# Seven sub-products of a gated layer in another order, passes of 6, 8 and 8 tiles, and one subtraction moved from VectorE to GpSimd

## What is computed

```python
def trunk(x, ...):
    for l in range(DEPTH):                                  # DEPTH = 2
        x = x + 0.5 * swiglu(rmsnorm(x, norm_g[l, 0]), ffn_w_gu[l, 0], ffn_w_down[l, 0])
        xn = rmsnorm(x, norm_g[l, 1])
        y, ns = even_mixer(xn, ...) if l % 2 == 0 else odd_mixer(xn, ...)
        x = x + y
        x = x + 0.5 * swiglu(rmsnorm(x, norm_g[l, 2]), ffn_w_gu[l, 1], ffn_w_down[l, 1])
    return rmsnorm(x, final_norm_g), new_states

def swiglu(x, w_gu, w_down):                                # 1024 -> 2 x 2816 -> 1024
    g, u = jnp.split(x @ w_gu, 2, axis=-1)
    return (jax.nn.silu(g) * u) @ w_down
```

## Time and profile before

| | |
|---|---|
| median of 3 runs | 2731.59 us (2727.64 to 2732.09) |
| the profiled execution | 2732.55 us, span 2730.8 us |
| mean granted TensorE clock | 0.959 |
| PE / VectorE / ScalarE / GpSimd busy | 94% / 60% / 35% / 29% of the span |
| an undisturbed up-tile | 12.31 us |

### The profile page before, as it was taken

How to read it: one execution, slowest core, us unless ns; L and a number is a source line. 1 busy time by engine, 2 the same in 40 slices (tenths; PEclk the granted TensorE clock), 3 DMA queues, 4 the chain that set the end, 5 groups by cost and what they waited for, 6 DMA issues and landing times. The chain is left out here.

```text
span 2730.8 us, 46499 instructions
## 1 busy us (share of the span) xinstructions
PE 2563.3 (94%) x18787; PEld 2420.3 (89%) x18787; DVE 1651.9 (60%) x2986; ACT 960.4 (35%) x1640; POOL 793.4 (29%) x434
## 2 busy tenths in 40 slices
PE   4999999999789999999799999999888898999997
PEld 4999999998659999999799999999844488999997
DVE  7848579322345867758884857931133348848486
ACT  4414333220173433424441433321054544424242
POOL 1232323321152232333223232332233331232322
PEclk7999999999599999999899999999988999999998
DMA  3222222222351222222222222234599931222222
GB/s 110 70 86 78 78 93 63 79 76 84 127 224 63 77 70 89 76 92 66 74 70 85 78 78 93 65 111 127 215 360 369 368 141 49 76 93 70 85 71 77
DMA packets 66556, 304.20 MB, mean 111 GB/s; under 512 B 9361, under 2 KB 13218, under 8 KB 40242
## 3 DMA queue, kind: packets, MB, share of 16 engines
q1 hardware_dynamic: 66354, 301.38, 31.7%
HBM read 279.95 MB, written 21.41 MB: 110 GB/s over the span
## 5 line engine op out<-in xcount | busy, mean ns | idle before, releaser
L782 PE MATMUL ps<-xs_hi,wb_hi 128*128 128x320 f32 x2112 | 664.7, 315 | 62.3 <-DVE xs_lo L607 32.1
L782 PE MATMUL ps<-xs_lo,wb_hi 128*128 128x320 f32 x2112 | 659.6, 312 | 0.0
L782 PE MATMUL ps<-xs_hi,wb_lo 128*128 128x320 f32 x2112 | 659.5, 312 | 0.0
L362 POOL TENSOR_TENSOR w_lo<-w_raw,w_hi 128x1024 fp32r<-128x1024 f32 (+2 forms) x130 | 393.6, 3030 | 655.5 <-ACT w_hi L358 655.5
L665 POOL TENSOR_TENSOR wb_lo<-w_raw,wb_hi 128x512 fp32r<-128x512 f32 x176 | 281.4, 1601 | 954.8 <-DVE wb_lo L673 656.6
L782 PEld LDWEIGHTS ps<-xs_hi,wb_hi 128*128 128x128 f32 x2112 | 402.8, 191 | 71.8 <-DVE xs_lo L607 29.5
L782 PEld LDWEIGHTS ps<-xs_lo,wb_hi 128*128 128x128 f32 x2112 | 403.3, 191 | 0.0
L782 PEld LDWEIGHTS ps<-xs_hi,wb_lo 128*128 128x128 f32 x2112 | 403.0, 191 | 0.0
L358 ACT ACTIVATE w_hi<-w_raw 128x1024 fp32r<-128x1024 f32 (+2 forms) x130 | 158.2, 1217 | 585.7 <-PE ps L376 504.2
L376 PE MATMUL ps<-h_hi,w_hi 128*128 128x320 f32 x1408 | 321.3, 309 | 2.4 <-DVE h_lo L939 2.0
L376 PE MATMUL ps<-h_lo,w_hi 128*128 128x320 f32 x1408 | 320.8, 309 | 0.0
(11 more groups left out here) (241 smaller groups left out, 4365.6 us busy)
## 6 DMA issues: line engine op xcount, KB each, us to landing
w_raw<-in_w_up SPq DMA_DIRECT2D x87, 1024.0 KB, 4.8
kv_ring<-in_fox_kc SPq DMA_DIRECT2D x32, 1024.0 KB, 12.8
...
```

The costliest lines, as they stand in the source:

```text
L362: nc.gpsimd.tensor_tensor(out=w_lo[:, slot, 0:cols], in0=w_raw[:, slot, 0:cols], in1=w_hi[:, slot, 0:cols].bitcast(F32), op=ALU.subtract). ...
L782: last = nc.tensor.matmul(ps[:, bank, 0:HALF], w_part[:, slot, cols], x_part[:, k, :], start=k == 0 and i == 0, stop=k == 3 and i == 2)
```

## The change

`PRODUCTS` becomes P1, P5, P2, P3, P6, P7, P4. The passes have 6, 8 and 8 tiles. The low part of A12 is made on GpSimd. In `ffn_dve` a tile now begins with P4's eviction and `prod*gate` of the tile ahead; S4 of the next tile is formed and reduced one tile ahead, right behind each other; the gate's chain ends inside the tile, so ScalarE's silu comes there too. The diagonal and the copy to `inv_rms` move from VectorE to ScalarE. In the boundaries S1, S2 and S4 with S1's low part (`first_blocks_dve`) are made behind x tiles 4, 5 and 6, the rest (`late_blocks_*`) inside the last x tile, between its first and second low part. In the first layer the eight squares are no longer summed by VectorE: PE sums them in 40 matmuls of one column behind P5. In other layers `ffn_stats` comes behind P3 instead of P6. `sum_x` and `inv_rms` move to other places in SBUF, masks are cast behind the first pass, and x is loaded ahead of the first weight block. The number of other matmuls and the bytes loaded are the same.

```diff
-GROUPS = ((0, 8), (8, 16), (16, 22))
+GROUPS = ((0, 6), (6, 14), (14, 22))
-PRODUCTS = ("P1", "P5", "P6", "P2", "P7", "P4", "P3")
+PRODUCTS = ("P1", "P5", "P2", "P3", "P6", "P7", "P4")
...
+READ_AT = {"P2": 1, "P6": 2, "P3": 4, "P7": 5, "P5": 6, "P4": 7}
...
-    def second_lo_step(dve, ph, t):
+    def second_lo_step(pool, ph, t):
...
-        nc.vector.tensor_tensor(out=wb_lo[:, slot, :], in0=raw_part(n, "A12"), in1=wb_hi[:, slot, :].bitcast(F32),
+        nc.gpsimd.tensor_tensor(out=wb_lo[:, slot, :], in0=raw_part(n, "A12"), in1=wb_hi[:, slot, :].bitcast(F32),
...
+    def first_blocks_dve(dve, ph, t, step):
+        if step == 0:
+            sum_step(dve, ph, t, "S1")
+        elif step == 1:
+            sum_step(dve, ph, t, "S2")
+        else:
+            sum_step(dve, ph, t, "S4")
+            sum_lo_step(dve, ph, t, "S1")
+    def late_blocks_dve(dve, ph, t):
+        sum_lo_step(dve, ph, t, "S4")
+        sum_lo_step(dve, ph, t, "S2")
+        sum_step(dve, ph, t, "S3")
+        sum_lo_step(dve, ph, t, "S3")
...
     def ffn_stats(pe, ph):
         r = ph["norm"]
         if r == 0:
             pe.wait_ge(consts_loaded, 16 * len(consts))
+            pe.wait_ge(sq_done, KT)
+            for tt in range(TT):
+                for m in range(KT):
+                    last = nc.tensor.matmul(ps[:, STATS_BANK, tt:tt + 1], first_squares[:, m, tt * P:(tt + 1) * P],
+                                            mean_model[:, :], start=m == 0, stop=m == KT - 1)
...
-                    if t == 0 and name == "P6":
+                    if t == 0 and name == ("P3" if ph["norm"] else "P5"):
                         ffn_stats(pe, ph)
...
             for t in range(lo, hi):
+                plain_lo_step(pool, ph, t, "A22")
+                if t + 1 < hi:
                     plain_lo_step(pool, ph, t + 1, "A11")
+                    second_lo_step(pool, ph, t + 1)
...
                 if t > lo:
-                    second_half(t - 1)
+                    up_first(t - 1)
+                    hidden(t - 1)
                 if more:
                     sum_step(dve, ph, t + 1, "S1")
-                sum_lo_step(dve, ph, t, "S4")
+                    sum_step(dve, ph, t + 1, "S2")
+                    sum_lo_step(dve, ph, t + 1, "S1")
...
+                take(t, "P2", 1, gate[:, t % 2, 0:HALF], part[:, 0, :], None)
+                if t == 0:
+                    ffn_norm_dve(dve, ph)
+                if t > lo:
+                    hidden_lo(t - 1, lo)
                 if more:
+                    sum_step(dve, ph, t + 1, "S4")
+                    sum_lo_step(dve, ph, t + 1, "S4")
...
+                take(t, "P6", 2, part[:, 1, :], part[:, 0, :], None)
+                take(t, "P5", 3, part[:, 2, :], part[:, 1, :], 2)
+                take(t, "P3", 4, gate[:, t % 2, HALF:T], part[:, 2, :], 3)
...
+                nc.vector.tensor_tensor(out=gate[:, t % 2, :], in0=gate[:, t % 2, :], in1=inv_rms[:, :],
+                                        op=ALU.mult).then_inc(gate_ready, 1)
                 if more:
                     sum_step(dve, ph, t + 1, "S3")
                     sum_lo_step(dve, ph, t + 1, "S2")
...
-                take(t, "P7", part[:, 1, :], part[:, 1, :], 2)
+                take(t, "P7", 5, part[:, 1, :], part[:, 1, :], 3)
...
                 if more:
                     sum_lo_step(dve, ph, t + 1, "S3")
-                    second_lo_step(dve, ph, t + 1)
...
+            nc.scalar.activation(gate[:, 1, tt * P:(tt + 1) * P], ident[:, :], ACT.Copy,
+                                 scale=rs[1][:, tt:tt + 1]).then_inc(diag_done, 1)
```

More of the change, by code:

```diff
@@ L162, in trunk_program @@
     tile_b = T * 4
-    inv_rms = place("inv_rms", [P, T], F32, at_e + 7 * tile_b)
+    at_inv = (end - tile_b) // 64 * 64
+    inv_rms = place("inv_rms", [P, T], F32, at_inv)
     xs = [[(place(f"xs_hi{e}", [P, 6, 4, HALF], F32R, at_xs[e]),
@@ L528, in raw_part @@
         return w_raw[:, n % 2, c0:c0 + BLOCK]
+    SUM_AT = {"S1": 1, "S2": 2, "S4": 3, "S3": 4}
+    SUM_LO_AT = {"S1": 1, "S4": 2, "S2": 3, "S3": 4}
+    PLAIN_AT = {"A11": 1, "A12": 2, "A22": 3}
     SUMS = {"S1": sum_x, "S2": sum_y, "S3": sum_x, "S4": sum_z}
@@ L568, in lo_before, with xs_dve @@
         return 16 * ph["index"] + 2 * pos
-    def xs_dve(dve, ph, m, pos):
+    def xs_dve(dve, ph, m, pos, between=None, scaled=None):
+        scaled = prod[:, 0, :] if scaled is None else scaled
         r = ph["norm"]
@@ L693, in block_prep_late_act @@
         sum_hi_step(act, ph, t, "S2", used, count)
[L694 removed]
         sum_hi_step(act, ph, t, "S3", used, count)
[L696 to L703 removed]
+    FIRST_BANK = tuple(0 if hi - lo == 8 else 4 for lo, hi in GROUPS)
+    STATS_BANK = (FIRST_BANK[0] + 6) % 8
     def bank_of(ph, t, name):
@@ L858, in ffn_act @@
             r = ph["norm"] + 1
+            follow = (nxt, 0) if last else (ph, hi)
+            blocks = not last or (nxt is not None and nxt["kind"] == "ffn")
             for d in range(KT):
@@ L927, in take, with up_first @@
             nc.vector.tensor_tensor(out=dst, in0=src, in1=bank(t, name), op=ALU.add).then_inc(evicted, 1)
-        def second_half(t):
-            u = f0 + t
-            take(t, "P3", gate[:, t % 2, HALF:T], part[:, 2, :], 2)
-            dve.wait_ge(evicted, 7 * u + 7)
-            nc.vector.tensor_tensor(out=gate[:, t % 2, :], in0=gate[:, t % 2, :], in1=inv_rms[:, :],
-                                    op=ALU.mult).then_inc(gate_ready, 1)
+        def up_first(t):
+            take(t, "P4", 7, prod[:, t % 2, 0:HALF], part[:, 1, :], 5)
         def hidden_lo(t, lo):
@@ L997, in ffn_dve @@
             r = ph["norm"] + 1
+            follow = (nxt, 0) if last else (ph, hi)
+            blocks = not last or (nxt is not None and nxt["kind"] == "ffn")
             if last:
                 clear_sum(dve)
+            if ph["index"] == 0 and g_ == 0:
+                cast_masks(dve)
             for d in range(KT):
                 q = q0 + d
-                if d == KT - 1 and not last:
-                    block_prep_dve(dve, ph, hi)
-                elif d == KT - 1 and nxt is not None and nxt["kind"] == "ffn":
-                    block_prep_dve(dve, nxt, 0)
+                late = (lambda: late_blocks_dve(dve, *follow)) if d == KT - 1 and blocks else None
                 dve.wait_ge(unit_ready, q + 1)
@@ L2061, in _ @@
     def _(pool):
[L2062 removed]
+        plain_lo_step(pool, PLAN[0], 0, "A11")
+        second_lo_step(pool, PLAN[0], 0)
         for ph in PLAN:
@@ L2084, in _, with square @@
         act.wait_ge(gains_loaded, 16)
-        for m in range(KT):
-            if m == 4:
-                sum_hi_step(act, PLAN[0], 0, "S1")
-                block_prep_late_act(act, PLAN[0], 0, None, 0)
+        two = lambda m: prod[:, m % 2, :]
+        def square(m):
+            nc.scalar.activation(first_squares[:, m, :], x_res[:, m, :], ACT.Square).then_inc(sq_done, 1)
+        for m in range(4):
             act.wait_ge(x_loaded[m // 2], 16)
             xs_act(act, PLAN[0], m, m)
-        for m in range(KT):
-            nc.scalar.activation(first_squares[:, m, :], x_res[:, m, :], ACT.Square).then_inc(sq_done, 1)
+            square(m)
+        sum_hi_step(act, PLAN[0], 0, "S1")
+        plain_hi_step(act, PLAN[0], 0, "A12")
+        late_blocks_act(act, PLAN[0], 0, None, 0)
+        for m in (4, 5):
+            act.wait_ge(x_loaded[2], 16)
+            xs_first(act, PLAN[0], m, two(m), 0)
+            square(m)
+        for m in range(4, KT):
+            xs_second(act, PLAN[0], m)
+            if m < KT - 2:
+                act.wait_ge(x_loaded[3], 16)
+                xs_first(act, PLAN[0], m + 2, two(m), lo_before(PLAN[0], m) + 1)
+                square(m + 2)
         for ph in PLAN:
```

327 lines of the change are left out of this document (154 added, 173 removed).

## The result

The changed kernel takes **2820.22 us** (median of 4, 2819.98 to 2820.79), the kernel before 2730.95 (2727.64 to 2732.09): a ratio of 1.0329, 95% interval 1.0311 to 1.0347. The direction was forecast, the size was not: 2790 was predicted, and the range ended at 2812.

The account below looks back on a forecast made before the run. TensorE was taken as the bound (busy 2563.3 of 2730.8 us), with VectorE setting the pace in late up-tiles. 2732.5 + 99 - 7 - 4 - 28 = 2792.5, so 2790 was forecast, range 2690 to 2812.

Parts of the forecast that it names:

- Part 1: Steady up-tiles: VectorE held by GpSimd, tile 13.9 us against 12.31; +99 over four layers, -7 for today's excess.
- three exclusions: Late up-tiles: GpSimd operations hold up low S3 (+0.94), `prod*gate` (+0.6) and `h_lo` (+0.8).
- The stall at S4: Steady tile: S4's low part right behind S4 waits for ScalarE's rounding, a VectorE stall of 0.78.
- (a): Rival: GpSimd's operations fall into VectorE's waits and evictions, tile under 12.31, total 2693; chance 0.22.
- (b): Rival: one of the three exclusions is hidden, tile 12.6 to 13.3, total 2738 (2700 to 2765); chance 0.16.
- (c): Rival: all three exclusions cost 1.15, tile 15.0, total 2863; chance 0.05.
- Part 2: Last down-pass: eight tiles make the last hidden tile due later and silu earlier, 1.0 in each of four, -4.
- Part 3: First tiles of the four layers with the gap ahead: second -6.4, fourth -8, third -10, first -3; together -28 (-20 to -40).
- By the durations above: Second layer's first tile: steps timed from earlier durations, ending at 899.1 against 905.53, -6.4.
- The gap ahead of the third layer: Ahead of the third layer's first tile: units of 7.04 leave VectorE less behind, gap 5.4 (between 0 and 9.10).
- Costed at nothing: Items put at zero: x loaded ahead of the first block, masks cast later, moved sum tiles, down loads cut differently.
- Rival (d): Start of the first layer: the 40 sums hold PE longer, at most 17 us, inside part 3's bounds; no chance given.

Follow-up runs that it names:

- experiment 4: Experiment 3's kernel with `h_lo` between S4 and its low part, instead of behind both: 2718.17 us, ratio 0.996.
- experiment 1: Changed kernel with GpSimd's three subtractions per up-tile cut to 16 columns, except in a pass's first and a layer's second tile: 2716.46 us.
- experiment 3: Changed kernel with GpSimd's operation on A12 held until behind S4's low part, beside evictions: 2761.76 us.
- experiment 9: Experiment 8's kernel with GpSimd's A11 operation behind S4's low part and its A12 operation behind S2's low part: 2701.06 us, ratio 0.989.
- experiment 6: Changed kernel with GpSimd's three subtractions cut to 16 columns in each layer's second tile only: 2812.48 us.
- experiment 8: Experiment 7's kernel with GpSimd's A22 and A11 subtractions of a layer's first tile held until the norm's chain is done: 2710.82 us, ratio 0.9927.
- Experiment 7: Experiment 4's kernel with the first weight block loaded ahead of x, as in the kernel before: 2717.78 us, ratio 0.9949.
- experiment 10: First layer's squares summed block by block as they come: on experiment 9's kernel 2690.61 us, ratio 0.9852; alone in the changed kernel 2815.19.

## Why the prediction was wrong

**Part 1, the steady tile, had the mechanism and the size of a tile right.** Forecast 13.9, measured 13.87; PE third in the tile behind P5's second reading; three exclusions of 0.9, 0.6 and 0.7 at the places named; a pass of eight 11.0 longer than 98.5 (forecast 10.5). The stall at S4 was forecast as 0.78, and experiment 4 took out 0.72. Experiments 1, 3, 4 and 9 show the cause. Per layer it was 26.8 instead of 24.8. Later passes lose 1.67 already in their second tile, where I had put 1.05 (one loses 3.8 there), and the first passes lose 4.0 to 5.2, where I had put 3.8. With the 8.6 of today's excess, which I had at 7, part 1 is +98.5 for +92. Rivals (a), (b) and (c) fall: none of the three was hidden, none cost the full 1.15.

The rule of the Trainium skill that I had weighed, in "SBUF — State Buffer", section "SBUF: two separate sides" (whoever holds the shared pair keeps it for a whole instruction), is borne out: `prod*gate` and S1 grow by up to 1.09 beside a GpSimd operation of about 1.3, and evictions from PSUM not at all. The row of 2519.39 in the earlier trace rows, where the GpSimd operation starts 0.04 ahead of VectorE's and is yet the one drawn out, shows that two starts so close don't tell who comes first. The price of a whole operation for each of the three, which I had worked out beside it, was too high: 2.2 in all, not 3.8.

**Part 2** was right: -3.8 for -4.

**Part 3, the first tiles, is the step that failed**: -28 forecast (its four terms add up to -27.4), -2.5 measured, 25.5 of the miss of some 28 against the forecast's sum. That this is nearly all of the miss is luck: the 6.5 of part 1 and the -5.9 of the mixers cancel. Two of its steps were wrong:

- "By the durations above": for the second to fourth layer I took the durations of rows in which VectorE is alone and wrote out the order on PE only. In the new order S1, S2 and low S1 stand between the last x and P2's eviction with the norm's chain behind it, and three GpSimd operations start in that very stretch. The exclusion that I had costed three times in the steady tile was left out here, where it costs 3.1 ahead of the chain in each layer. PE's wait moved from the activations' low parts to the spread, and behind that wait its clock fell once more, which costs another 1.3 to 2.6 in the spread and P4; I had the half clock behind the statistics alone. Experiments 6 and 8 give 4.4 and 5.4 of the two together back in the second layer, 3.3 and 4.3 in the third: 22.07 and 22.90 where I had 20.6 and 21.6. The gap ahead of the third layer, forecast 5.4, was 6.34. The remaining 1.5 in the second layer lies ahead of all this: the square sum is there 11.7 us into the tile, where I had 9.3, in the changed kernel and in experiment 8 alike, so GpSimd isn't its cause; the statistics give 0.8 of that back (1.3 for 2.1). Why the sum comes so late no run took apart.
- "Costed at nothing: x loaded ahead of the first block (PE needs both)". That PE needs both is true, but the block was the later one: PE started at 9.70 instead of 8.03. The sums took 17.20 (forecast 17.1) but began at 32.17, not 29.4, and the tile ended at 62.72, not 59.4. Experiment 7 gives 1.75 of the start back, 0.8 at the tile's end. Rival (d), the sums holding PE, had the right place: experiment 10 gives 10.2 to 12.5 back there.

The range failed for the same reason: -20 to -40 for part 3 had no row in it in which GpSimd is busy in the boundary. With 0 as its upper bound, for which the earlier trace rows gave cause (L632 drawn out to 1.77 there already), the range would have held 2820. It was also narrower than its own bounds: 2732.5 + 115 - 7 - 4 - 20 is 2816.5, not 2812.

**A version that beats both.** The order of the change with GpSimd's operations placed, `h_lo` between S4 and its low part, the first load as before, and the squares summed as they come takes 2690.61: 1.5% under the kernel before and 4.6% under the changed one.
